# Time-step and gate projections with stationary weights in column groups

## The reference, cut to what matters

```python
def hybrid_mixer(hn, w_in, ...):                 # hn: 256 x 1024, already normed
    proj = hn @ w_in
    z, xbc, dt_raw, qkv = split(proj)            # dt_raw: 256 x 8
    dt = softplus(dt_raw + dt_bias)
    y = ssd_chunked(xh, dt, a, bm, cm)           # everything of the recurrence needs dt
...
def nsa_attention(h, w_in, ...):
    ..., g = split(h @ w_in)                     # g: 256 x 48
    gates = sigmoid(g)
    return gates[0] * o_c + gates[1] * o_s + gates[2] * o_w
```

## Time and profile before

| | |
|---|---|
| median of 3 runs | 1044.87 us (1044.31 to 1045.33) |
| span of the profiled execution | 1038.8 us |
| PE busy | 1012.5 us, 97% of the span |
| DVE / ACT / POOL busy | 748.5 / 522.9 / 145.3 us |
| DMA | 169.71 MB, mean 163 GB/s |

### The profile page before, as it was taken

How to read it: one execution, slowest core, us unless ns; L and a number is a source line. 1 busy time by engine, 2 the same in 40 slices (tenths; PEclk the granted TensorE clock), 3 DMA queues, 4 the chain that set the end, 5 groups by cost and what they waited for, 6 DMA issues and landing times. The chain is left out here.

```text
span 1038.8 us, 22480 instructions
## 1 busy us (share of the span) xinstructions
PE 1012.5 (97%) x8555; PEld 960.4 (92%) x8555; DVE 748.5 (72%) x1198; ACT 522.9 (50%) x900; POOL 145.3 (14%) x194
## 2 busy tenths in 40 slices
PE   8999999999999999989999999999998999999998
PEld 8999788999999998858999999998986699999998
DVE  5876887656666666884777777778967677777776
ACT  6453665644444454226644444456745565444442
POOL 0070010011222100002000010040115600001000
PEclk9999999999999999999999999999999999999999
DMA  9563235266565646641655656655730045655651
GB/s 353 164 200 100 61 109 176 92 201 189 190 200 195 194 138 190 188 124 62 183 186 203 198 186 199 199 169 141 245 119 21 1 139 170 203 197 185 199 189 75
DMA packets 51042, 169.71 MB, mean 163 GB/s; under 512 B 5665, under 2 KB 10785, under 8 KB 50849
## 3 DMA queue, kind: packets, MB, share of 16 engines
q1 hardware_dynamic: 45216, 163.22, 49.0%
q10 hardware_dynamic: 5760, 5.57, 2.0%
HBM read 162.15 MB, written 1.05 MB: 157 GB/s over the span
## 5 line engine op out<-in xcount | busy, mean ns | idle before, releaser
L1566 DVE TENSOR_TENSOR WL<-WR,WH 128x1024 fp32r<-128x1024 f32 x302 | 373.6, 1255 | 139.1 <-ACT WH L1299 136.7
L861 PE MATMUL acc<-XH,WH 128*128 128x256 f32 x1360 | 385.1, 283 | 3.1 <-DVE XP L1583 2.0
L862 PE MATMUL acc<-XL,WH 128*128 128x256 f32 x1360 | 376.4, 277 | 0.0
L863 PE MATMUL acc<-XH,WL 128*128 128x256 f32 x1360 | 376.4, 277 | 0.0
L1299 ACT ACTIVATE WH<-WR 128x1024 fp32r<-128x1024 f32 x302 | 310.9, 1051 | 69.2 <-PE acc L863 37.8
L861 PEld LDWEIGHTS acc<-XH,WH 128*128 128x128 f32 x1360 | 255.5, 188 | 7.1 <-DVE WL L1566 3.7
L862 PEld LDWEIGHTS acc<-XL,WH 128*128 128x128 f32 x1360 | 255.7, 188 | 0.9
L863 PEld LDWEIGHTS acc<-XH,WL 128*128 128x128 f32 x1360 | 255.5, 188 | 0.0
L861 PE MATMUL big<-UH,WH 128*128 128x256 f32 x608 | 167.9, 276 | 0.0
L863 PE MATMUL big<-UH,WL 128*128 128x256 f32 x608 | 167.8, 276 | 0.0
L862 PE MATMUL big<-UL,WH 128*128 128x256 f32 x608 | 167.8, 276 | 0.0
(11 more groups left out here) (301 smaller groups left out, 1362.2 us busy)
## 6 DMA issues: line engine op xcount, KB each, us to landing
WR<-weights SPq DMA_DIRECT2D x302, 512.0 KB, 3.7
STK<-UP ACTq DMA_DIRECT2D x32, 138.0 KB, 3.6
X<-x_t SPq DMA_DIRECT2D x4, 256.0 KB, 6.1
MEM<-mem_t SPq DMA_DIRECT2D x1, 1024.0 KB, 9.7
result_t<-X SPq DMA_DIRECT2D x4, 256.0 KB, 2.2
CON<-constants SPq DMA_DIRECT2D x1, 880.0 KB, 12.8
CBUF<-KCV ACTq DMA_DIRECT2D x4, 128.0 KB, 5.3
CBUF<-KCV ACTq DMA_DIRECT2D x4, 127.5 KB, 6.2
```

The source lines that it names most:

```text
L861: pe.matmul(out, wh, hi, start=start, stop=False, skip_group_check=True)
L862: pe.matmul(out, wh, lo, start=False, stop=False, skip_group_check=True)
L863: return pe.matmul(out, wl, hi, start=False, stop=stop, skip_group_check=True)
L1566: dve.tensor_tensor(WL[:, cs % SPL], WR[:, cs % RAW], WH[:, cs % SPL].bitcast(F32), ALU.subtract).then_inc(w_low, 1)
```

## The change

Both narrow products swap their operands: the weights become stationary, padded from 8 to 32 and from 48 to 64 columns, and G moves, all 256 tokens at once. Feature tiles are spread over column groups of the array: four groups of 32 for the time steps, two of 64 for the gates, each adding its own share of the features in its own partitions of PSUM. The shares are copied to SSUM (by ACT for the time steps, by DVE for the gates), and a product with a 0/1 matrix (`sum32`, `sum64`) adds the groups and turns the result token-major, into the place where the old one stood. In PE's order the sum of the time steps stands behind the transpose of line 988 and ahead of `mem_key(0)`; the sum of the gates stands behind `head_sums(0)`. In DVE's order `gate_inputs`, which now also copies, moves from step 1 to step 0, ahead of `positions(1)`. CON grows by 56 columns, SML by 320.

```diff
-          ("v_mask", 128), ("ident4", 32), ("cos", T), ("sin", T)]
+          ("v_mask", 128), ("ident4", 32), ("cos", T), ("sin", T), ("sum32", 8), ("sum64", 48)]
...
-SMALLS = [("w_dt", 8 * 8), ("w_gate", 8 * 48), ("ck_w2", 2 * P), ("cv_w2", 2 * P)]
+SMALLS = [("w_dt", 8 * 32), ("w_gate", 8 * 64), ("ck_w2", 2 * P), ("cv_w2", 2 * P)]
...
             pe.wait_ge(sem("g_ready"), 16)
-            for tt in range(TT):
-                for k in range(KD):
-                    ins = pe.matmul(big[:, 3, 64 * tt:64 * tt + 48], G[:, k, tt * P:tt * P + P],
-                                    small("w_gate")[:, k * 48:k * 48 + 48], start=k == 0, stop=k == KD - 1,
-                                    skip_group_check=True)
-            ins.then_inc(sem("gate_ps"), 1)
+            for i in range(4):
+                for g in range(2):
+                    k = 2 * i + g
+                    ins = pe.matmul(big[64 * g:64 * g + 64, 3, T:2 * T], small("w_gate")[:, 64 * k:64 * k + 64], G[:, k, :],
+                                    start=i == 0, stop=i == 3, skip_group_check=True)
+            ins.then_inc(sem("gate_parts"), 1)
+
+            def sum_gates():
+                pe.wait_ge(sem("gate_copied"), 1)
+                for tt in range(TT):
+                    ins = pe.matmul(big[:, 3, 64 * tt:64 * tt + 48], SSUM[:, tt * P:tt * P + P], con("sum64"), start=True,
+                                    stop=True, skip_group_check=True)
+                ins.then_inc(sem("gate_ps"), 1)
...
                 if n >= 2:
                     rotate(n - 2)
+                if n == 1:
+                    sum_gates()
...
                 dve.tensor_scalar(RSN[:, :], RST[:, :], -1.0, None, ALU.mult).then_inc(sem("rsn_done"), 1)
+                dve.wait_ge(sem("gate_parts"), 1)
+                dve.tensor_copy(SSUM[:, :], big[:, 3, T:2 * T]).then_inc(sem("gate_copied"), 1)
...
                 if n == 0:
+                    gate_inputs()
                     positions(1)
-                if n == 1:
-                    gate_inputs()
...
             pe.wait_ge(sem("g_ready"), 8)
-            for tt in range(TT):
-                for k in range(KD):
-                    ins = pe.matmul(mis[:, 1, tt * 8:tt * 8 + 8], G[:, k, tt * P:tt * P + P],
-                                    small("w_dt")[:, k * 8:k * 8 + 8], start=k == 0, stop=k == KD - 1,
-                                    skip_group_check=True)
-            ins.then_inc(sem("dt_ps"), 1)
+            for i in range(2):
+                for g in range(4):
+                    k = 4 * i + g
+                    ins = pe.matmul(mis[32 * g:32 * g + 32, 1, T:2 * T], small("w_dt")[:, 32 * k:32 * k + 32], G[:, k, :],
+                                    start=i == 0, stop=i == 1, skip_group_check=True)
+            ins.then_inc(sem("dt_parts"), 1)
...
             pe.transpose(big[:, 3, 256:384], XB[:, 4, 0:P], con("ident")).then_inc(sem("bt_ps"), 1)
+            pe.wait_ge(sem("dt_copied"), 1)
+            for tt in range(TT):
+                ins = pe.matmul(mis[:, 1, tt * 8:tt * 8 + 8], SSUM[:, tt * P:tt * P + P], con("sum32"), start=True, stop=True,
+                                skip_group_check=True)
+            ins.then_inc(sem("dt_ps"), 1)
             mem_key(0)
...
             act.preload_act_table_set("natural_log_exp_and_others")
+            act.wait_ge(sem("dt_parts"), 1)
+            act.activation(SSUM[:, :], mis[:, 1, T:2 * T], ACT.Copy).then_inc(sem("dt_copied"), 1)
             act.wait_ge(sem("dtr_done"), 1)
```

More of the change, by code:

```diff
@@ L2169, in _constants @@
         "ident4": np.repeat(np.eye(32), 4, axis=0), "cos": cos, "sin": sin,
+        "sum32": i[:, None] % 32 == np.arange(8)[None, :], "sum64": i[:, None] % 64 == np.arange(48)[None, :],
     }
@@ L2252, in by_tile, with wider @@
         return w.reshape(k, P, -1).transpose(1, 0, 2).reshape(P, -1)
+    def wider(w, n):
+        return np.concatenate([w, np.zeros((w.shape[0], n - w.shape[1]), w.dtype)], axis=1)
     gate_cols = np.concatenate([nsa[7][:, 3 * h:3 * h + 3] for h in order], axis=1)
-    smalls = np.concatenate([by_tile(dt), by_tile(gate_cols), by_tile(np.tile(a["nsa_ck_w2_2"][0], (1, 2))),
+    smalls = np.concatenate([by_tile(wider(dt, 32)), by_tile(wider(gate_cols, 64)), by_tile(np.tile(a["nsa_ck_w2_2"][0], (1, 2))),
                              by_tile(np.tile(a["nsa_cv_w2_2"][0], (1, 2)))], axis=1)
```

## The result

The changed kernel takes 1049.27 us (median of nine executions, 1048.53 to 1051.05); the kernel before, beside it, 1045.22 us. The ratio is 1.0049, with a 95% interval from 1.0036 to 1.0063: slower, by 4 us between the medians and 5 by the ratio, where 3.5 us less was forecast. One of the nine executions of the kernel before took 1688.22 us and is left out of the ratio. The span of the profiled execution is 1047.7 us, and its own time is 2.0 us longer than its span. So it is, to 0.1 us, in all profiled runs listed here. By that, of the 6.0 us by which the median before stood above the span before, some 4 were the distance from a short execution to the usual one (but for that one execution, the kernel before ranges from 1040 to 1048 us in all these runs).

A forecast was written before the change was run, and what follows sets the result against it. PE, busy for 97% of the span, was taken as the bound. Gains of 3.5 (time steps), 0 (gates) and 0 (start) take the span from 1038.8 to 1035.3; with the median's 6.0 us excess kept, 1041.4 us, range 1039.7 to 1043.2.

The forecast's parts named there:

- the sum, 3.5 + 0 + 0: Gains forecast at the time steps, the gates and the start (larger CON and SML loads), in us.
- the sixth rival: Tiles behind CON and SML move 1504 bytes; down products on UH and UL slow, 8.2 us lost, 1049.6 us; 6%.
- the sign by which it showed: Sign of a wrong forecast: pieces of lines 861 to 863 further apart in the feed-forward loops.
- PE's work at the time steps: Time-step products: shares take 1.10 us instead of 3.50, the sum adds 0.45; net 1.95 us less.
- The copy: Time steps: ACT's 0.47 us copy to SSUM ends near 83.4, PE asks at 84.4, so it is hidden.
- The waits behind: Behind the time steps: result ready about 85.1, CBM ends near 90.35, line 1001 reached at 91.05 without waiting.
- The clock near 86 us: Behind the time-step products: the low clock (0.50) was expected to be gone, 1.55 us less.
- The rival drawn from the Trainium skill: Between shares and `mem_key(0)`: transposes and small products still bring the low clock, 1.6 us lost, 1043.0 us; 15%.
- Gates at nothing: Gates: PE has 1.15 us less work but waits 1.65 us instead of 0.49 at the second `head_sums`; gain 0.
- the first rival: Gates: the time is kept because CBUF copies land earlier, up to 1.15 us more gained, 1040.2 us; 12%.
- The low stretch near 465 us: Low clock from 464.83 us taken as unchanged; rival: it meets other work or none, up to 1.6 us better; 5%.
- Later stages carry the gain on: Behind the time steps: stages wait on one another, not on a fixed time, so 3.5 us carries to the end.

The follow-up runs named there:

- the move alone: The kernel before with an unused buffer of 376 columns behind the small weights, moving every tile behind by 1504 bytes: 1052.55 us, ratio 1.0078.
- the moved change: The changed kernel with an unused buffer of 8 columns (32 bytes) behind the small weights: 1040.35 us, ratio to the kernel before 0.9967.
- the two halves: The changed kernel with the old gates, and with the old time steps, each with 32 bytes behind SML: 1039.28 us (0.9957) and 1043.44 us (1.0002).

## Why the prediction was wrong, point by point

The step that failed is the layout: the sum, 3.5 + 0 + 0, has no term for it, and the sixth rival gives it 6%. In its place the runs showed 9.2 us by the traces, 8.6 by the ratios of the change and of the same moved by 32 bytes, 8.1 for the move alone. The rival's price was near, 8.2 us on the 1824 products and 1049.6 us against 1049.27 measured, but in part by luck. (The 1824 products themselves make 7.1 us, at 3.9 ns each; the rest are products on XH just behind a run on UH, the first six of which keep the longer spacing.) The 0.118 us behind the price was read off two tiles on XH, which the change does not move and whose longer spacing stays unexplained; and 5.74 us for 48 is 0.120, by which the price would have been 11.9 us. What was wrong above all is the chance of 6%, and the reason for it, that nothing shows that addresses set the pace. The trace of before couldn't show it, since no address varies within it. But the reason answered nothing: two spacings stood in that trace without a cause, and the addresses, had they been read beside it, have all the moving operands (XH, YH, UH, UL) at the same distance from the weights modulo 256 (the period is known only from the runs), which the change took from one pair alone. The kernel's text had a sign too: ahead of WR it declares a tile `shift_back` of 320 bytes that nothing reads, without which XH and YH would stand at a distance of 0. A rival with a known price of more than twice the gain and no row against it deserved a far larger share, and a range that reached it. The prediction did name the sign by which it showed, pieces of lines 861 to 863 further apart in the feed-forward loops.

- **PE's work at the time steps**: right. The shares took 1.00 us and 0.09 for going in (1.10 forecast), the sum 0.37 (0.45).
- **The copy**: hidden, as said. SSUM stands at 84.89, and PE asks at 86.19. The warning of the Trainium skill, TensorEngine Tiling (Array Packing), section PSUM Bottleneck, would have made the gain 3.0; the trace gave 3.5.
- **The waits behind**: right to 0.1 us. DTR begins 3.38 us after the first product (forecast 85.1 - 81.69 = 3.41), CBM ends after 8.62 (8.66), L1016 begins after 9.31 (9.36) and waits for nothing.
- **The clock near 86 us**: its price was right, its certainty not. Without the fall, eight transposes and what follows up to the ninth wide product take 88.71 - 85.97 = 2.74 us in the kernel with the gates alone, against 4.25 before: 1.51 us, 1.55 forecast. But of eight profiled executions with the old products the clock fell in seven, for 3.41 us in five and 6.83 in two; in three with the new ones it never fell. So about 1.5 us of the 3.5 is what an execution usually gains, not always. That the pieces of 8 columns cause the fall is likely, not shown. The rival drawn from the Trainium skill, TensorE: Matmul & The Clock Gate, Part 4: PE-mode transpose, by which transposes count less as work for the clock, found no support in those three, whose transposes are the same.
- **Gates at nothing**: right, 1.0002 alone, by the mechanism given. The wait was 2.02 and 2.13 us, 1.65 forecast, as the DMA came 0.4 us later than before. In the moved change's trace it came 0.9 us earlier and PE kept 0.85, the first rival in part. (The old wait stood 9.6 us behind the end of the gate products, not behind their beginning: 710.79 against 701.22.)
- **The low stretch near 465 us**: was taken as fixed but for a rival of 5%. It lasts 3.41 or 6.83 us, or isn't there at all, also where nothing but the layout differs from the kernel before (none with the move by 256 bytes, 6.83 us with that by 128).
- **Later stages carry the gain on**: right where the spacing held. In the moved change PE's lead over the trace of before doesn't alter through any of the three loops.

## What to carry to other kernels

A change that makes any SBUF tile larger moves every tile behind it: work out the new start of each streamed operand against its stationary one, modulo 256 bytes here, and pad back to the old distance, or time the move by itself before judging the change. A rival that no row contradicts and whose price exceeds the gain needs a chance to match, even without a mechanism. And an engine's saved time counts only up to the next thing that it waits for: at the gates 1.2 us of PE's work bought nothing, because a DMA set the date.

## What the hardware showed that was not expected

- In this kernel's second and third feed-forward loops, back-to-back products of 256 fp32r columns settle at starts 113 ns apart when the moving operand starts 64 bytes short of a multiple of 256 behind the stationary one, and at 117 to 119 ns at the five other distances tried (0, 64, 160 and 224 behind on UH, 128 on XH). The moves that put UH and UL at the other distances cost 8 to 12 us of the kernel's time, the one that did it to the more numerous products on XH, XL, YH and YL some 24 us.
- The longer spacing is also found at the good distance. It lasts over two to six products behind a run at the longer spacing; in the first loop, with UH and UL moved by 128 bytes, over whole runs on XH. Between 48 and 70 us, ahead of any product on UH, products on XH at a distance of 192 keep 113 ns in four traces (before, moved by 256, and the two halves) and 118 in six, the moved change among them. So the distance is not all that counts; what else does stays open.
- Low clock stretches differ between profiled executions that do the same work there: near 465 us 3.41 us in the kernel before, none when it was moved by 256 bytes, 6.83 when it was moved by 128. Near 790 us ten of the eleven traces have one of 3.41 or 6.83 us, that of before none; in the change's it costs nothing that lasts, since PE is 6.04 us behind the trace of before ahead of it and 6.05 after it. The first rise came between 4.03 and 7.29 us after the start of the span.
